# First mixer of a two-block kernel: query and key units ahead of the value units, small fp32 products in 32-partition strips

## What is computed

```python
q = rms_norm(q.reshape(bsz, seq, ATTN_HEADS, HEAD_DIM), q_norm_g[layer])
k = rms_norm(k.reshape(bsz, seq, ATTN_HEADS, HEAD_DIM), k_norm_g[layer])
attn = stick_breaking_attention(q, k, v).reshape(bsz, seq, ATTN_WIDTH)
c = glu_a * jax.nn.sigmoid(glu_b)
c = causal_depthwise_conv(c, conv_dw_w[layer], conv_dw_b[layer])
c = jax.nn.silu(layer_norm(c, conv_ln_g[layer], conv_ln_b[layer]))
mixed = jnp.concatenate([attn, c], axis=-1) @ w_out[layer]
```

## Time and profile before

| | |
|---|---|
| median of three executions | 1272.07 us (1269.72, 1272.07, 1273.02) |
| the profiled execution | 1268.72 us, its span 1267.0 us |
| mean granted TensorE clock | 0.982 of 2.4 GHz |
| TensorE products busy | 1227.4 us, 97% of the span |
| VectorE busy | 590.4 us, 47% |
| ScalarE busy | 480.8 us, 38% |
| GpSimd busy | 512.4 us, 40% |

### The profile page before, as it was taken

How to read it: one execution, slowest core, us unless ns; L and a number is a source line. 1 busy time by engine, 2 the same in 40 slices (tenths; PEclk the granted TensorE clock), 3 DMA queues, 4 the chain that set the end, 5 groups by cost and what they waited for, 6 DMA issues and landing times.

```text
span 1267.0 us, 15300 instructions
## 1 busy us (share of the span) xinstructions
PE 1227.4 (97%) x5681; PEld 992.3 (78%) x5681; DVE 590.4 (47%) x846; ACT 480.8 (38%) x698; POOL 512.4 (40%) x289
## 2 busy tenths in 40 slices
PE   7999979999999999999999998999999999999997
PEld 6876737788888888888877777887888888888886
DVE  5686965235544444100264586973444444440003
ACT  6232644434333333222355644343343333332122
POOL 3631111345443444444583232226344444344442
PEclk8998978999999999999999999999999999999999
DMA  5420110123323232222313111122232323322211
GB/s 172 133 100 5 62 34 31 36 100 100 99 86 105 74 102 97 100 99 99 100 58 118 50 52 34 34 67 67 67 121 78 101 98 99 116 100 100 100 67 66
DMA packets 84598, 105.39 MB, mean 83 GB/s; under 512 B 2019, under 2 KB 77130, under 8 KB 84554
## 3 DMA queue, kind: packets, MB, share of 16 engines
q1 hardware_dynamic: 84394, 104.53, 24.9%
q10 hardware_dynamic: 160, 0.26, 0.1%
HBM read 102.43 MB, written 2.10 MB: 82 GB/s over the span
## 4 chain that ended last, share of the span: by engine, by line
PE 80%; DVE 6%; issue 5%; POOL 4%; ACT 3%; DMA 1%; SPq 0%; POOLq 0%; ACTq 0%; DVEq 0%
PE ps L1491 16%; PE ps L1492 15%; PE ps L1493 15%; PE ps L1788 9%; PE ps L1793 9%; PE ps L1575 4%; PE ps L1969 3%; POOL w_lo L426 3%; PE ps L1922 2%; DVE cy L1055 2%; PE ps L1617 1%; PE ps L1592 1%; DVE sp_lo L1090 1%; PE ps L1602 1%; DVE zl L1086 1%
## 5 line engine op out<-in xcount | busy, mean ns | idle before, releaser
L426 POOL TENSOR_TENSOR w_lo<-w_raw,w_hi 128x1024 fp32r<-128x1024 f32 x180 | 433.5, 2411 | 616.6 <-ACT w_hi L549 615.5
L1491 PE MATMUL ps<-h_hi,w_hi 128*128 128x512 f32 x936 | 371.3, 397 | 3.2 <-POOL w_lo L426 1.8
L1492 PE MATMUL ps<-h_lo,w_hi 128*128 128x512 f32 x936 | 365.4, 390 | 0.0
L1493 PE MATMUL ps<-h_hi,w_lo 128*128 128x512 f32 x936 | 365.1, 390 | 0.0
L549 ACT ACTIVATE w_hi<-w_raw 128x1024 fp32r<-128x1024 f32 x190 | 200.0, 1055 | 328.1 <-PE ps L1493 145.4
L1491 PEld LDWEIGHTS ps<-h_hi,w_hi 128*128 128x128 f32 x936 | 176.4, 188 | 44.9 <-issue 5.6
L1493 PEld LDWEIGHTS ps<-h_hi,w_lo 128*128 128x128 f32 x936 | 176.2, 188 | 37.3
L1492 PEld LDWEIGHTS ps<-h_lo,w_hi 128*128 128x128 f32 x936 | 176.4, 189 | 35.3 <-issue 0.5
L1181 DVE TENSOR_TENSOR ps<-ps,rbs 128x512 f32<-128x512 f32 x88 | 61.5, 699 | 172.0 <-PE ps L1493 171.6
L726 ACT ACTIVATE cv<-ps,par 128x512 f32<-128x512 f32 x44 | 34.3, 780 | 183.9 <-DVE ps L1181 161.9
L1147 DVE TENSOR_TENSOR xT<-xT,ps 128x512 f32<-128x512 f32 x24 | 16.3, 684 | 154.9 <-PE ps L1793 106.7
(11 more groups left out here) (276 smaller groups left out, 1701.2 us busy)
## 6 DMA issues: line engine op xcount, KB each, us to landing
w_raw<-in_w_up SPq DMA_DIRECT2D x33, 1024.0 KB, 5.1
w_raw<-in_w_down SPq DMA_DIRECT2D x22, 1024.0 KB, 4.8
w_raw<-in_w_in SPq DMA_DIRECT2D x21, 1024.0 KB, 5.2
w_raw<-in_w_gate SPq DMA_DIRECT2D x11, 1024.0 KB, 5.1
w_raw<-in_w_out SPq DMA_DIRECT2D x8, 1024.0 KB, 4.9
xtok<-in_x SPq DMA_DIRECT2D x4, 512.0 KB, 5.3
out_dram<-obuf SPq DMA_DIRECT2D x8, 256.0 KB, 2.1
sq<-in_final_norm_w SPq DMA_DIRECT2D x1, 512.0 KB, 5.9
```

The source lines that it names most:

```text
L426: pool.tensor_tensor(unit_view(w_lo, at, down), unit_raw(at, down), unit_view(w_hi, at, down).bitcast(F32), ALU.subtract).then_inc(s_lo, 1)
L1491: pe.matmul(ps[:, bank, :], whi, hi, start=first, stop=False, skip_group_check=True)
L1492: pe.matmul(ps[:, bank, :], whi, lo, start=False, stop=False, skip_group_check=True)
L1493: mm = pe.matmul(ps[:, bank, :], wlo, hi, start=False, stop=last, skip_group_check=True)
```

## The change

1. **Order of the units.** Queries and keys of heads 4 to 7 become units 12 to 15, the values units 16 to 19 (the loads swap accordingly). Units 12 to 15 go to banks 6 and 7 between statistics, scores and tails of heads 0 to 3; the four value products follow in banks 7 and 6 between the heads (`value_rows`), one of them cut in two by scores(4, 5).
2. **Strips.** The selector has 32 columns and each of the four statistics products writes its own 32 partitions; the inverse root is kept on 128 partitions; a spread takes its 32 rows of them and writes a bank of its own (the four of the first group banks 0 to 3, the second group banks 7 and 6 by turns). The mean is four products with 32 columns, each into its own 32 partitions, a VectorE copy of the bank, and one 128x128 product with 1/32. The sums of squares go the same way with a ScalarE copy, and then four products with one column. The selector's transpose selT is now made by TensorE and copied by VectorE; a memset and two selects on GpSimd go.
3. **Scores of heads 6 and 7** are made together, after the last tap; tails(4), tails(5) and outputs(0) stand ahead of it.
4. **Tiles.** Heads 4 and 5 keep their scores where queries and keys of heads 0 to 3 were, so front(4) no longer waits for outputs(0).
5. **ScalarE and VectorE** follow in their orders; the leads of w_out's first four units (20 to 23) stand around weights(4).

```diff
+SCALED = (4, 6, 5, 7, 0, 2, 1, 3)
+SCALE_BANK = (0, 1, 2, 3, 7, 6, 7, 6)
+VALUE_BANK = (7, 6, 7, 6)
...
-            sel = sb("sel", [P, 8, 16], stack=early)
-            selT = sb("selT", [16, 8, P], stack=early)
-            nvar = sb("nvar", [16, 3, SEQ], stack=early)
-            lnone = sb("lnone", [P, P], stack=early)
+            sel = sb("sel", [P, 4, 32], stack=early)
+            selT = sb("selT", [P, P], stack=early)
...
+        def zslot(h):
+            if h in (4, 5):
+                return qk[:, 4:9, :].rearrange("p a n -> p (a n)")[:, (h - 4) * ZW:(h - 3) * ZW]
+            return zl[:, h % 6 if h >= 6 else h, :]
...
-            in_cols = [B0, A0, B0 + 256, A0 + 256, 0, 512, V0, V0 + 256, 256, 768]
+            in_cols = [B0, A0, B0 + 256, A0 + 256, 0, 512, 256, 768, V0, V0 + 256]
...
             for u in range(8, 12):
                 take_qk(u, u % 4)
-                lead(u + 4)
+                if u < 11:
+                    lead(u + 4)
                 square_qk(u, u + 1)
+            lead(15)
             table(6)
             scale_root(0)
-            for t in range(TT):
-                value(t)
+            take_qk(12, 6)
             lead(16)
+            act.wait_ge(s_qst, 1)
+            square_qk(12, 13)
+            take_qk(13, 7)
             lead(17)
+            square_qk(13, 14)
             front(0)
             front(1)
+            take_qk(14, 6)
             lead(18)
+            square_qk(14, 15)
+            weights(0)
+            take_qk(15, 7)
+            square_qk(15, 16)
             lead(19)
-            take_qk(16, 7)
-            act.wait_ge(s_qst, 1)
-            square_qk(16, 13)
-            weights(0)
-            take_qk(17, 6)
-            square_qk(17, 14)
             weights(1)
+            scale_root(1)
             front(2)
             front(3)
-            take_qk(18, 7)
-            square_qk(18, 15)
-            take_qk(19, 6)
-            square_qk(19, 16)
+            value(0)
+            value(1)
             weights(2)
+            weights(3)
+            front(4)
+            front(5)
+            value(2)
+            value(3)
             lead(20)
             lead(21)
-            scale_root(1)
-            weights(3)
+            weights(4)
+            lead(22)
+            lead(23)
+            weights(5)
             attended_hi(0)
-            front(4)
-            front(5)
+            front(6)
             attended_hi(1)
-            weights(4)
-            weights(5)
-            front(6)
             front(7)
-            act.wait_ge(s_qst, 2)
...
+            weights(6)
             attended_hi(2)
-            lead(22)
-            weights(6)
-            lead(23)
+            act.wait_ge(s_lp, 1)
...
-                w = gq8[:, 0:1] if j < 4 else par[:, 0, C_KG:C_KG + 1]
+                j = SCALED[n]
+                w = gq8[:, 0:1] if j in Q_TILE else par[:, 0, C_KG:C_KG + 1]
                 dve.wait_ge(s_qb, n + 1)
-                dve.scalar_tensor_tensor(qk[:, j, :], qk[:, j, :], w, ps[:, 4 + 2 * g + n % 2, :],
+                dve.scalar_tensor_tensor(qk[:, j, :], qk[:, j, :], w, ps[:, SCALE_BANK[n], :],
                                          ALU.mult, ALU.mult).then_inc(s_qn, 1)
             def head(h):
...
+            taps(1, 0, 2)
             scale_variance(0)
-            taps(1, 0, 1)
+            taps(1, 2, 3)
             scale_refine(0)
-            taps(1, 1, 4)
+            taps(1, 3, 4)
             dve.wait_ge(s_cdve, 5)
             for n in range(4):
                 scale_qk(n)
-            taps(1, 4, 14)
+            taps(1, 4, 10)
             head(0)
             head(1)
-            taps(1, 14, 23)
+            taps(1, 10, 14)
+            scale_variance(1)
+            taps(1, 14, 15)
+            scale_refine(1)
+            taps(1, 15, 16)
             head(2)
             head(3)
-            taps(1, 23, 26)
-            scale_variance(1)
-            taps(1, 26, 27)
-            scale_refine(1)
+            taps(1, 16, 19)
             scale_qk(4)
-            attended_lo(0)
             scale_qk(5)
+            taps(1, 19, 21)
             scale_qk(6)
             scale_qk(7)
-            taps(1, 27, CK)
+            taps(1, 21, 26)
             head(4)
             head(5)
+            taps(1, 26, CK)
+            attended_lo(0)
+            dve.wait_ge(s_lp0, 1)
+            dve.tensor_copy(nvar[:, 0, :], ps[:, 6, :]).then_inc(s_lpd, 1)
             dve.wait_ge(s_mean, 1)
             for c in range(CT):
                 dve.tensor_tensor(cy[:, c, :], cy[:, c, :], ps[:, 6, :], ALU.subtract).then_inc(s_lc, 1)
+            head(6)
             attended_lo(1)
-            head(6)
             head(7)
...
             def statistics(g, bank):
-                for n, u in enumerate(range(8 + 8 * g, 12 + 8 * g)):
-                    pe.wait_ge(s_qsq, 4 * g + n + 1)
-                    mm = pe.matmul(ps[0:16, bank, :], sel[:, QK_TILE[u], :], sqk(n), start=(n == 0), stop=(n == 3))
+                pe.wait_ge(s_qsq, 4 * g + 4)
+                for n in range(4):
+                    mm = pe.matmul(ps[32 * n:32 * n + 32, bank, :], sel[:, n, :], sqk(n), start=True, stop=True,
+                                   skip_group_check=True)
                 mm.then_inc(s_qst, 1)
             def spread_scale(n):
-                g, j = n // 4, GROUPS[n // 4][n % 4]
+                g, row = n // 4, 32 * (SCALED[n] % 4)
                 pe.wait_ge(s_qv, 5 * g + 5)
-                if n % 4 >= 2:
+                if n >= 6:
                     pe.wait_ge(s_qn, n - 1)
-                pe.matmul(ps[:, 4 + 2 * g + n % 2, :], selT[:, j, :], nvar[:, 1, :], start=True, stop=True).then_inc(s_qb, 1)
+                elif n >= 4:
+                    pe.wait_ge(s_vc, n - 3)
+                pe.matmul(ps[:, SCALE_BANK[n], :], selT[row:row + 32, :], nvar[row:row + 32, 1, :],
+                          start=True, stop=True, skip_group_check=True).then_inc(s_qb, 1)
...
+            def value_rows(t, ks=range(KD)):
+                if ks[0] == 0:
+                    pe.wait_ge(s_lo, 20)
+                    if t == 0:
+                        pe.wait_ge(s_take, 16)
+                    elif t == 1:
+                        pe.wait_ge(s_qv, 6)
+                    else:
+                        pe.wait_ge(s_qn, 5 + t)
+                values(t, s_vt, ks, VALUE_BANK[t])
+            def channel_sums(weight, src, sem):
+                for c in range(CT):
+                    mm = pe.matmul(ps[32 * c:32 * c + 32, 6, :], weight, src(c), start=True, stop=True,
+                                   skip_group_check=True)
+                mm.then_inc(sem, 1)
+            pe.wait_ge(s_tap, 2 * CK)
+            part(12, 6, range(4))
             statistics(0, 4)
-            pe.wait_ge(s_lo, 16)
-            for t in range(TT):
-                pe.wait_ge(s_take, 8 + t + 1)
-                values(t, s_vt)
-                if t == 1:
-                    for n in range(4):
-                        spread_scale(n)
+            part(12, 6, range(4, 8))
+            part(13, 7, range(4))
+            pe.wait_ge(s_cdve, 6)
+            for n in range(4):
+                spread_scale(n)
+            part(13, 7, range(4, 8))
             pe.wait_ge(s_qn, 4)
-            pe.wait_ge(s_vc, 4)
-            pe.wait_ge(s_cdve, 4)
             scores((0, 1))
-            pe.wait_ge(s_tap, 2 * CK)
-            part(16, 7, range(8))
-            part(17, 6, range(4))
+            pe.wait_ge(s_take, 13)
+            part(14, 6, range(8))
+            pe.wait_ge(s_take, 14)
+            part(15, 7, range(4))
             tails(0)
-            part(17, 6, range(4, 8))
+            part(15, 7, range(4, 8))
             tails(1)
-            pe.wait_ge(s_take, 13)
-            part(18, 7, range(2))
+            pe.wait_ge(s_take, 15)
+            statistics(1, 6)
             scores((2, 3))
-            part(18, 7, range(2, 8))
-            pe.wait_ge(s_take, 14)
-            part(19, 6, range(8))
+            value_rows(0)
+            value_rows(1)
             tails(2)
-            pe.wait_ge(s_take, 16)
-            statistics(1, 6)
+            spread_scale(4)
+            spread_scale(5)
             tails(3)
-            outputs(0)
-            spread_scale(4)
-            pe.wait_ge(s_mlo, 1)
-            spread_scale(5)
-            pe.wait_ge(s_qn, 6)
-            scores((4, 5))
             spread_scale(6)
             spread_scale(7)
+            value_rows(2, range(4))
             pe.wait_ge(s_qn, 8)
-            outputs(1)
-            pe.wait_ge(s_tap, 4 * CK)
-            for c in range(CT):
-                mm = pe.matmul(ps[:, 6, :], lnone[:], cy[:, c, :], start=(c == 0), stop=(c == CT - 1))
-            mm.then_inc(s_mean, 1)
+            scores((4, 5))
+            value_rows(2, range(4, 8))
+            value_rows(3)
             tails(4)
             tails(5)
-            scores((6,))
-            scores((7,))
```

(40 more changed lines are left out.)

45 lines of the change are left out of this document (24 added, 21 removed).

## The result

The changed kernel took **1255.09 us** (median of 4 runs, 1253.82 to 1258.94) beside 1271.07 for the kernel before (4 runs, 1269.72 to 1273.02): ratio 0.9878, 95% interval 0.9863 to 0.9893, so 13.6 to 17.4 us less. 1257 was predicted. The profiled execution took 1255.25 us with a span of 1253.5, against 1267.0 before.

A forecast was written before the change was run, and what follows sets the result against it. TensorE bounds the kernel (80% of the chain of waits); in the changed stage VectorE's order decides until the last tap, TensorE's after. -2.5 and -11.1 give -13.6 from 1268.7: 1255.1, plus 2.2 is 1257 us (68%); range 1240 to 1268.

The forecast's parts named there:

- The rival with strips that don't overlap: Groups of four strips take the 3.6 us of one by one; kernel at 1269, same as before; chance 12%.
- From 84.9 to the last tap: Stage's first stretch, from unit 11's end: last tap at 185 us against 187.5, so -2.5 us.
- neither has slack, and each delay of one lengthens the stretch: Before the last tap, TensorE's work sums to 76.5 us and VectorE's to 75.9, ending at 161.4 and 161.5.
- work of VectorE: Up to the last tap: 62 taps 40.9, six heads 22.8, scalings, refinings and variance 12.2; 75.9 us.
- waits 3: VectorE waiting for others before the last tap: 0.8 for first statistics, 1.7 for front(4), some 3 us together.
- clock 3: After TensorE's long wait for head(0), done near 116.5, work at 1.2 GHz costs some 3 us.
- the rests: Eight GpSimd rests of w (16 to 23) beside second-half taps and heads hold VectorE 2.2 us each: 17.6 us.
- The first rival, rests that hardly hurt: Most rests fall in VectorE's waits; last tap at 165 to 170, stage gains 28 to 33 us: 1241; chance 15%.
- no low clock after the first spreads: Sign that the forecast is right: the granted clock is not low once the first spreads are done.
- From the last tap on: Last tap to stage's end: TensorE's work and waits in order sum to 35.4 us, before 46.5; -11.1 us.
- tails(6): TensorE's tails of head 6, after the last tap and behind the wait for head(6): 2.75 us.
- The 2.2 us added: Mean of four executions of the kernel before lies 2.2 us above the profiled one; added to 1255.1, giving 1257.

The follow-up runs named there:

- experiment 2: Changed kernel with the strips of the two channel sums one after the other, each product waiting for the one before; 1262.92 us, ratio 0.9943 to the kernel before.
- experiment 3: Changed kernel with the strips of the two statistics and of the spreads one after the other; 1262.68 us, ratio 0.9942 to the kernel before.
- experiment 12: Changed kernel with all its strips (statistics, spreads, both channel sums) one after the other, new order kept; 1269.64 us against 1268.43 for the kernel before, ratio 1.0006.
- experiment 4: Changed kernel with GpSimd's rests of weight units 16 to 23 computed for only 16 numbers a partition; 1238.94 us, ratio 0.9756 to the kernel before.
- experiment 8: Kernel before with one edit alone: scores of heads 6 and 7 as a pair instead of two singles; 1271.79 us against 1268.74, ratio 1.0020.
- late leads: Changed kernel with ScalarE's leading parts of weight units 20 to 23 behind a wait for the last tap; 1246.45 us, ratio 0.9828 to the kernel before.
- experiment 1: Changed kernel with the mean of the channels as before: four accumulating 128-column products, no 1/32 product or bank copy; 1258.67 us, ratio 0.9924 to the kernel before.
- experiment 5: The late leads: changed kernel with ScalarE's leads of units 20 to 23 behind a wait for the last tap; 1246.45 us, ratio 0.9828 to the kernel before.
- experiment 6: Changed kernel with scores of heads 6 and 7 ahead of the wait for the last tap; 1253.49 us, ratio 0.9886 to the kernel before.
- experiment 7: Changed kernel with leads of units 20 to 23 behind the last tap and scores((6, 7)) ahead of its wait; 1248.18 us, ratio 0.9832 to the kernel before.
- experiment 11: Changed kernel with 40 extra 512-column products on TensorE ahead of its wait for the last tap; 1255.72 us, ratio 0.9895 to the kernel before.

## Why the prediction was right

**Strips.** 0.95 us was taken for a group of four; 0.99 to 1.14 was measured. By the factors of the Trainium skill (TensorE: Matmul & The Clock Gate, Part 3) the estimate was 1.2 to 1.5. Four products of 0.94 us in 0.99 are 3.8 times by columns, and in 1.14 they are 3.3 times by rows, where the Trainium skill has 3.07 for four row strips; the measurement decides. The rival with strips that don't overlap is out by experiments 2, 3 and 12.

**From 84.9 to the last tap.** Predicted 185, measured 182.0. The sum's form holds: "neither has slack, and each delay of one lengthens the stretch" is what experiments 3 (TensorE) and 4 (VectorE) show. Its terms: work of VectorE 75.9 predicted, and 91.4 busy less 14.9 of stretching and 0.9 of the gate is 75.6; waits 3 and clock 3 predicted, 6.3 of idle time found (97.7 less 91.4), most of it a wait of 4.2 before head(4), where 1.7 had been laid out. The stage began 0.4 us earlier, which is chance (in experiment 8, the kernel before up to there, it began 1.4 us earlier).

**The mis-sized term is the rests**: 8 x 2.2 = 17.6 predicted, 14.9 found as 2.2 (16) + 0 (17) + 2.1 (18) + 2.2 (19) + 8.4 (20 to 23). Rest 17 met twelve taps in a row and was itself the one held: it took 6.82 us for 2.4. So the taps did not end near 110 but at 107.8, head(0) was done at 112.3 instead of 116.5, and TensorE's long wait for it, to which the clock term was pinned, did not come. The clock fell all the same in two other places: after the spreads (0.57 from 97 to 101), and at 148.4, where TensorE had been busy for 1.8 of the 4 us before. As an estimate, 6.8 us of work at half the clock cost 3.4 us, so the 3 us were found, but by another way, and "no low clock after the first spreads" was wrong. The 2.0 us of waiting ahead of those spreads, for the refinement that rest 16 had stretched, are not enough to explain the first of the two, as the traces under "Open" show. The first rival, rests that hardly hurt (1241), is out: the last tap is at 182.0 and not before 170, and only without the eight rests does the kernel take 1238.9.

**From the last tap on.** 35.4 predicted, 37.3 measured, 46.5 before. Channel sums 1.94 (1.9), scores and masks 4.1 (4.5), 1/32 product 1.07 (0.95), wait for head(6) 4.30 (4.2) came as summed. The missed term is tails(6): 2.75 predicted, 4.5 measured, much of it at the clock of 0.50 behind that wait. A wait of 4.3 us was in the sum, but its clock was not. Experiment 8 corrects a reading inside the -11.1: the pair of scores, priced at 1.2 to 2.6, gives nothing on its own in the old order.

**Where the gain came from.** The sum booked -2.5 and -11.1; the trace has -5.5 and -9.1. That its total fits to 0.1 us (13.5 for 13.6) is luck in part: 3.0 us booked too much ahead of the tap, 1.9 too little behind it, and the 1.1 of later stages cancel. The 2.2 us added to get from the trace to 1257 were right for the kernel before (2.4) and wrong for the new one, whose median lies at its profiled execution; so the gain by medians is 16.0 us and by ratio 15.5, both above the 13.6.

Experiments 2 and 3 take away 8.3 us behind the last tap and 8.1 ahead of it; together they undo the whole gain. One caution: one by one the strips are dearer than the old forms. Each statistics takes 4.3 us against 3.6, the first four spreads 5.7 (97.2 to 103.0) against 5.2, the two channel sums 6.3 and 4.3 against 5.7 and 3.8, and the 1/32 product (1.07) is new. That is some 4 us of TensorE's time, so the new order may have given a few us that the twelfth experiment hides.

What it did not give is large: rests 16 to 23 cost 15.5 us (experiment 4), and the late leads get back 6.4. Not all of that is new. Besides the cast and the six taps of the earlier trace rows, two more operations of the kernel before were stretched by rests (3.58 for 1.49, 2.82 for 1.4):

```profile
133.93 3.58 DVE L1090 TENSOR_TENSOR sp_lo<-zl,sp_hi 128x1280 fp32r<-128x1280 f32 x1
...
163.75 2.82 DVE L1055 SCALAR_TENSOR_TENSOR cy<-glu,par,cy 128x512 f32<-128x512 f32 x2
```

The four together are some 7.3 us, against 14.9 now.

**Open:** whether rest 17 or the taps win the lock was not tried by itself, but seven traces have the same program in this stretch (the change and experiments 1, 2, 5, 6, 7 and 11, up to the leads of unit 20), and all seven wait 2.0 us ahead of the first spreads. Two views of experiment 6 (scores early), the first beside the row of the change for 97 to 101:

```profile
97.00:101.00 4.00, 4.00 (x20) 2.65 (x20) 4.00 (x7) 1.26 (x2) 0.00 (x0) 1.00 0.00 0
```

```profile
115.50 0.67 PE L1648 MATMUL ps<-sp_hi,ntri 128*128 128x512 f32 x1 [4.38 <-DVE sp_lo L1107]
```

In the change and with the late leads (experiment 5) the clock fell there, unit 13 ended later, so did ScalarE's copy of it and the lead behind it, and rest 17 began 3.5 us after the twelve taps and was held. In the other five traces the clock stayed at 1.00 from 96 to 101, rest 17 began 1.9 us after the taps and held them (10.2 us for twelve), rest 18 held an sp_lo, TensorE waited 4.4 us for head(0), and the clock fell on tails(0). That is the course that the prediction had described. The two courses cost nearly the same: the last tap is at 182.0 in one, and at 181.8, 183.1, 182.7 and 185.8 in experiments 1, 2, 6 and 11, where the leads of units 20 to 23 are early too. So the last tap of single traces moves by up to 4 us, and this stretch is not to be compared more finely. What decides whether the clock falls behind the spreads, and which side wins, stays open.

## What to carry to other kernels

Small fp32 products that use 32 rows or columns of the array can be packed four abreast at about the price of one, and where they stand in a chain that goes to and fro between two engines, most of that reaches the end (8.1 of 11 us here), even if the engine idles later. Before an order is settled, look where GpSimd's two-input work falls: put it beside VectorE operations that read PSUM or beside VectorE's idle time. Of a wait that stays, also count the lower clock of what follows it.

## What had not been expected of the hardware

- The lock between GpSimd and VectorE goes both ways. A rest of 2.4 us that began inside a run of twelve two-input SBUF taps took 6.82 us and left the taps at 0.67 each (8.04 for twelve). It had begun 3.5 us after the first of them; where it began 1.9 us after the first, the twelve took 10.17 and the rest 2.43.
- An operation of VectorE with one input in PSUM was not slowed beside a rest: four subtractions in 2.48 us with rests running (late leads), and in 2.48 us without.
- A cast with its one input in SBUF was slowed beside a rest (2.94 and 1.79 us for 0.83).
- A group of four fp32 products of 128x32 in strips is eight instructions, two for each product. The first four start within some 0.02 us (87.20 and 87.21 in the rows), the second four 0.44 us later (87.65 and 87.66), and the group ends after 0.99 us, with 32x128 after 1.14.
